# A two-layer hybrid model on one core: the modulation of the second layer beside the grouped attention, and three edits in the scan, its seam and the merge's gates

## What is computed

```python
def adaln(cond, ada_w, ada_b):
    m = jax.nn.silu(cond) @ ada_w + ada_b
    return jnp.split(m, 3, axis=-1)

def modulate(x, gain, shift, scale):
    return rms_norm(x, gain) * (1 + scale) + shift
```

## Time and profile before

| | us |
|---|---|
| median of three runs | 3320.42 |
| lowest, highest | 3320.09, 3335.84 |
| the profiled execution's own time | 3320.01 |
| its span | 3318.2 |
| TensorE busy | 2961.3 (89%) |
| VectorE busy | 1521.4 (46%) |
| ScalarE busy | 1090.3 (33%) |

### The profile page before, as it was taken

How to read it: one execution, slowest core, us unless ns; L and a number is a source line. 1 busy time by engine, 2 the same in 40 slices (tenths; PEclk the granted TensorE clock), 3 DMA queues, 4 the chain that set the end, 5 groups by cost and what they waited for, 6 DMA issues and landing times. The chain is left out here.

```text
span 3318.2 us, 55284 instructions
## 1 busy us (share of the span) xinstructions
PE 2961.3 (89%) x24050; PEld 2254.6 (68%) x24050; DVE 1521.4 (46%) x2488; ACT 1090.3 (33%) x1929; POOL 30.2 (1%) x28
## 2 busy tenths in 40 slices
PE   7799989989986898887899999799887988899998
PEld 3488766867854777445788787566655866788876
DVE  5623247354545344556454424355446435354522
ACT  5411367232253333212322123355323233332221
POOL 0000000000000010000000000000000000000000
PEclk9899999989968999788999998899888999999998
DMA  7511200123113111111233222421212122222321
GB/s 267 151 58 51 49 1 2 51 76 127 33 74 126 42 42 42 35 64 51 64 95 95 86 88 65 129 67 42 77 51 66 33 77 70 70 77 90 97 86 64
DMA packets 246083, 243.36 MB, mean 73 GB/s; under 512 B 28248, under 2 KB 216152, under 8 KB 245777
## 3 DMA queue, kind: packets, MB, share of 16 engines
q1 hardware_dynamic: 245538, 238.64, 23.1%
q10 hardware_dynamic: 304, 1.18, 0.1%
HBM read 217.03 MB, written 22.24 MB: 72 GB/s over the span
## 5 line engine op out<-in xcount | busy, mean ns | idle before, releaser
L201 DVE TENSOR_TENSOR second_w_low<-second_w_raw,second_w_high 128x1024 fp32r<-128x1024 f32 (+1 forms) x228 | 272.4, 1197 | 483.0 <-ACT second_w_high L197 482.4
L197 ACT CAST second_w_high<-second_w_raw 128x1024 fp32r<-128x1024 f32 (+1 forms) x228 | 233.0, 1024 | 689.5 <-PE ffn_in_acc L222 250.9
L220 PE MATMUL ffn_in_acc<-ffn_h_high,second_w_high 128*128 128x512 f32 x704 | 281.1, 399 | 13.9 <-DVE ffn_h_low L578 13.9
L222 PE MATMUL ffn_in_acc<-ffn_h_high,second_w_low 128*128 128x512 f32 x704 | 283.0, 402 | 0.0
L221 PE MATMUL ffn_in_acc<-ffn_h_low,second_w_high 128*128 128x512 f32 x704 | 279.7, 397 | 0.0
L201 DVE TENSOR_TENSOR first_w_low<-first_w_raw,first_w_high 128x1024 fp32r<-128x1024 f32 x115 | 140.1, 1222 | 266.4 <-ACT first_w_high L197 265.7
L197 ACT CAST first_w_high<-first_w_raw 128x1024 fp32r<-128x1024 f32 x115 | 120.2, 1047 | 233.2 <-PE attn_in_acc L222 80.9
L220 PEld LDWEIGHTS ffn_in_acc<-ffn_h_high,second_w_high 128*128 128x128 f32 x704 | 133.5, 190 | 47.8 <-issue 17.1
L220 PE MATMUL attn_in_acc<-attn_h_high,first_w_high 128*128 128x256 f32 (+1 forms) x416 | 144.3, 347 | 14.4 <-DVE attn_h_low L323 14.4
L221 PEld LDWEIGHTS ffn_in_acc<-ffn_h_low,second_w_high 128*128 128x128 f32 x704 | 133.7, 190 | 34.2 <-issue 0.5
L222 PEld LDWEIGHTS ffn_in_acc<-ffn_h_high,second_w_low 128*128 128x128 f32 x704 | 133.6, 190 | 31.1
(11 more groups left out here) (801 smaller groups left out, 6378.3 us busy)
## 6 DMA issues: line engine op xcount, KB each, us to landing
second_w_raw<-in_ffn_w_gate SPq DMA_DIRECT2D x44, 512.0 KB, 3.6
second_w_raw<-in_ffn_w_up SPq DMA_DIRECT2D x44, 512.0 KB, 3.6
second_w_raw<-in_ffn_w_down SPq DMA_DIRECT2D x40, 512.0 KB, 3.4
first_w_raw<-in_rec_w_in SPq DMA_DIRECT2D x33, 512.0 KB, 3.8
first_w_raw<-in_attn_ada_w SPq DMA_DIRECT2D x24, 512.0 KB, 4.7
first_w_raw<-in_rec_ada_w SPq DMA_DIRECT2D x24, 512.0 KB, 5.1
second_w_raw<-in_w_in SPq DMA_DIRECT2D x24, 512.0 KB, 3.7
second_w_raw<-in_w_branch_gate SPq DMA_DIRECT2D x24, 512.0 KB, 3.9
```

What stands on the lines that cost most here:

```text
L197: act.copy(self.view(self.high[b % self.splits], b), self.view(self.raw[b % self.bufs], b)).then_inc(self.high_done, 1)
L201: dve.tensor_tensor(self.view(self.low[b % self.splits], b), self.view(self.raw[b % self.bufs], b), self.view(self.high[b % self.splits], ...
L220: pe.matmul(out, sh, mh, start=(first and j == 0), stop=False)
L222: ins = pe.matmul(out, sl, mh, start=False, stop=(last and j == len(parts) - 1))
```

## The change

Four parts.

1. Only the first layer's adaLN stays in front, in one stage. Its 24 blocks are multiplied in plain f32, unsplit: the weights, 128 x 128, are stationary and silu(cond), two columns, moves; the result lies in PSUM as the modulation needs it. The second layer's 24 blocks ("rec_ada" in the stream, between the attention's input and output weights) are multiplied in the same way beside the grouped attention, one block in each of iterations 0 to 23; iteration 24 makes the first two splits of the output weights, and the modulation.
2. In the scan the square's products come out crossed (the two heads' halves swapped between partitions), so that the units are added by VectorE and not by TensorE; VectorE masks a crossed copy of the diagonal for GpSimd's first inverse, which is made in two halves; units of the later step ("ux") are added by VectorE; y is cleared by GpSimd.
3. At the seam before the scan, two of a unit's four saves are issued earlier, and the last unit's two later saves are waited for only ahead of the scan's second group.
4. The gates are kept in tanh form (g = tanh(a/2), the factor (g + 1) / 2). The eight `gates_first` are opened beside the delta scan, the four last tiles are made beside memory attention, the stage `merge_gates` is gone, and the delta branch's norm runs in `merge0`.

```diff
+def whole_product(pe, w, name, b, ps, silu):
+    b0, view = w.ranges[name][0], w.view(w.raw[b % w.bufs], b)
+    group = 4 * ((b - b0) // 4)
+    pe.wait_ge(w.landed[b % w.bufs], w.landings[b])
+    for j, k in enumerate(w.blocks[b][2]):
+        for i in range(4):
+            ins = pe.matmul(ps[:, group + i, :], view[:, j, i * P:(i + 1) * P], silu[:, k, :],
+                            start=(b == b0 and j == 0 and i == 0), stop=(k == KD - 1), skip_group_check=True)
+    ins.then_inc(w.used_whole, 1)
...
+def adaln(nc, w, cond, silu, layer, gains, aside):
...
+            for b in range(b0, b1):
+                whole_product(pe, w, "adaln", b, ps, silu)
+                aside.pe(pe, b - b0)
...
+            for b in first_splits(w, "attn_in"):
+                w.make_low(dve, b)
+            dve.wait_ge(w.used_whole, w.whole_upto[b1 - 1])
+            modulation(dve, chain, ps, *layer)
...
+class AdaLN:
...
+    def pe(self, pe, i):
+        if self.first + i < self.end:
+            whole_product(pe, self.w, "rec_ada", self.first + i, self.ps, self.silu)
...
+    def dve_last(self, dve, i):
+        if self.first + i == self.end:
+            for b in first_splits(self.w, "attn_out"):
+                self.w.make_low(dve, b)
+            dve.wait_ge(self.w.used_whole, self.w.whole_upto[self.end - 1])
+            modulation(dve, Chain(dve, self.own), self.ps, *self.layer)
...
-            attention(nc, "attn_grouped", pairs, gated(gb, qb), c["ident"])
+            attention(nc, "attn_grouped", pairs, gated(gb, qb), c["ident"], beside=beside)
...
             for n in range(n_units):
                 at = slice((n % 4) * P, (n % 4) * P + P)
+                sp.wait_ge(outs, n + 1)
+                for j in range(2):
+                    sp.dma_start(d["s_feat"][n // 4, j, at, :], out[n % 2][j]).then_inc(saved_out[n % 2], 16)
                 sp.wait_ge(features, n + 1)
...
             for i in range(3):
-                sp.wait_ge(saved_keys[i], 32 * len(range(i, n_units, 3)))
+                sp.wait_ge(saved_keys[i], 32 * len(range(i, n_units - 1, 3)))
...
             def square(n):
                 if n:
-                    pe.wait_ge(act_done, RWKV_ACT(n - 1, "way"))
-                constant(late, 0, all_of(units), 0)
...
+                    pe.wait_ge(act_done, RWKV_ACT(n - 1, "solved"))
+                pe.wait_ge(dve_done, RWKV_DVE(n, "diag"))
+                tiles(late, 0, dt, dn, 0, 1)
+                tiles(late, 256, dn, dt, 0, 1).then_inc(pe_done, 1)
...
             def sixteen(n):
                 pe.wait_ge(dve_done, RWKV_DVE(n, "eight"))
-                constant(early, 0, all_of(units))
                 pe.wait_ge(act_done, RWKV_ACT(n, "m2"))
-                tiles(late, 0, a8, m, 0, 0).then_inc(pe_done, 1)
+                tiles(late, 0, a8, m, 1, 0).then_inc(pe_done, 1)
...
+            def with_units(n, name, to, ps):
+                dve.wait_ge(pe_done, RWKV_PE(n, name))
+                for h in range(2):
+                    dve.tensor_tensor(to[:, :, h].rearrange("p a i t -> p a (i t)"),
+                                      bank(ps, h).rearrange("p (a t) -> p a t", a=2),
+                                      units.rearrange("p a i t -> p a (i t)"), ALU.add).then_inc(dve_done, 1)
...
                     masked(n, gb, "gram_b")
+                    with_units(n, "square", a2, late)
...
-                    odd_half(n, "ux", ux, early)
+                    with_units(n, "ux", ux, early)
...
-            attention(nc, "mem", pairs, [dict(out=branch[2][:, :, t * P:(t + 1) * P]) for t in range(4)], c["ident"], dims=P)
...
+                      beside=InPairs(Beside(w, "gates_last", *u, lambda e, n, ps: rooted(e, last_tile(n), ps, 0.5), 1, last_tile), 2))
...
-            linear(nc, "merge_gates", w, *u, S, lambda e, n, ps: rooted(e, gate(done + n), ps), engines="v",
...
-                ins = dve.tensor_tensor(g, g, ps[:, 0:S], ALU.mult)
+                ins = dve.scalar_tensor_tensor(out=g, in0=g, scalar=1.0, in1=ps[:, 0:S], op0=ALU.add, op1=ALU.mult)
```

More of the change, by code:

```diff
@@ L792, in act @@
             self.product.high(act, i // self.per)
+        if i % self.per == 0 and 1 <= i // self.per <= self.product.tiles and self.product.opened is not None:
+            self.product.treat(act, i // self.per - 1)
     def dve_first(self, dve, i):
@@ new lines, in modulation, with first_splits, _ @@
+def modulation(dve, chain, ps, bias, gain, mod, gs):
+    for j in range(2):
+        chain.link(dve.tensor_tensor(mod[:, :, j], ps[:, :, j], bias, ALU.add))
+        chain.link(dve.tensor_scalar(gs[:, :, j], mod[:, KD:2 * KD, j], 1.0, None, ALU.add))
+        chain.link(dve.tensor_tensor(gs[:, :, j], gs[:, :, j], gain, ALU.mult))
+def first_splits(w, name):
+    first = w.ranges[name][0]
+    return range(first, first + w.split_before(name))
+def adaln(nc, w, cond, silu, layer, gains, aside):
+    b0, b1 = w.ranges["adaln"]
+    with Stage(nc, "adaln") as st:
+        ps = st.ps("acc", [P, 24, 2])
+        silu_done, own = st.sem("silu_done"), st.sem("own")
+        aside.begin(st)
+        block = st.block()
+        @block.sync
+        def _(sp):
+            w.load_stage(sp, "adaln")
+        @block.tensor
+        def _(pe):
+            pe.wait_ge(silu_done, 1)
+            for b in range(b0, b1):
+                whole_product(pe, w, "adaln", b, ps, silu)
+                aside.pe(pe, b - b0)
+        @block.scalar
+        def _(act):
+            act.activation(silu, cond, ACT.Silu).then_inc(silu_done, 1)
+            for b in range(b0, b1):
+                aside.act(act, b - b0)
+            for b in first_splits(w, "attn_in"):
+                w.make_high(act, b, b, None, None)
+        @block.vector
+        def _(dve):
+            chain = Chain(dve, own)
+            dve.tensor_scalar(gains[0], gains[1], 0.125, None, ALU.mult)
+            for b in range(b0, b1):
+                aside.dve(dve, b - b0)
+            for b in first_splits(w, "attn_in"):
+                w.make_low(dve, b)
+            dve.wait_ge(w.used_whole, w.whole_upto[b1 - 1])
+            modulation(dve, chain, ps, *layer)
@@ L2512, in _ @@
             each = eye.rearrange("p (a t) -> p a t", a=1).broadcast_to([P, PAIRS, CH])
-            dve.memset(state[:], 0.0).then_inc(cleared, 1)
-            dve.memset(y[:], 0.0).then_inc(cleared, 1)
+            for dr in range(2):
+                dve.tensor_tensor(near[:, dr, :], chunk[:, 2 * dr, :], same, ALU.mult)
             dve.tensor_scalar(units[:, 0], each, -1.0, None, ALU.mult)
@@ L2518, in _ @@
                 dve.tensor_scalar(twice[:, h], each, 2.0, None, ALU.mult)
-            for dr in range(2):
-                ins = dve.tensor_tensor(near[:, dr, :], chunk[:, 2 * dr, :], same, ALU.mult)
-            ins.then_inc(cleared, 1)
-            dve.wait_ge(cleared, 3)
+            dve.memset(state[:], 0.0).then_inc(cleared, 1)
+            dve.wait_ge(cleared, 1)
             def near_diagonal(n):
@@ L2622, in _ @@
                 dr = groups[n][0]
-                for h in range(2):
-                    act.wait_ge(pe_done, RWKV_PE(n, f"square{h}"))
-                    half(n, "square", a2, late, h)
                 act.wait_ge(pe_done, RWKV_PE(n, "four"))
@@ L3932, in mixer @@
             kept = Ahead(nc, keep, "gates_kept")
-            kept.start(rest[:, 0:GATES_KEPT, :], d["s_gate"].rearrange("(i p) t -> p i t", p=P))
-            done = GATES_FIRST + GATES_KEPT
-            linear(nc, "merge_gates", w, *u, S, lambda e, n, ps: rooted(e, gate(done + n), ps), engines="v",
-                   then=lambda n: lambda act: act.activation(gate(done + n), gate(done + n), ACT.Sigmoid),
-                   aside=Asides(Opened([gate(i) for i in range(GATES_FIRST)], 2), NormAside(c, "dn_out", [branch[1][:, i, :] for i in range(4)], [v("dn_out_norm")] * 4,
-                                          c["pick_mean128"], spread[0:4, :], rs[0:4, :], [out[:, 5, :], out[:, 6, :]], normed,
-                                          dict(square=lambda i: i // 2, sum=lambda i: i // 2, root=1, inverse=1, apply=lambda i: 2 + i // 2),
-                                          finish=lambda dve, i: dve.tensor_tensor(branch[1][:, i, :], branch[1][:, i, :],
-                                                                                  zg[:, i, :], ALU.mult))))
+            kept.start(rest[:], d["s_gate"].rearrange("(i p) t -> p i t", p=P))
@@ new lines, in mixer @@
+            norm_out = NormAside(c, "dn_out", [branch[1][:, i, :] for i in range(4)], [v("dn_out_norm")] * 4,
+                                 c["pick_mean128"], spread[0:4, :], rs[0:4, :], [out[:, 5, :], out[:, 6, :]], normed,
+                                 dict(square=lambda i: i // 2, sum=lambda i: 1 + i // 2, root=3, inverse=3, apply=lambda i: 5 + i // 2),
+                                 finish=lambda dve, i: dve.tensor_tensor(branch[1][:, i, :], branch[1][:, i, :],
```

(3 more changed lines are left out.)

249 lines of the change are left out of this document (126 added, 123 removed).

## The result

The changed kernel takes 3369.14 us (median of four runs, 3358.14 to 3373.21) where the kernel before takes 3325.57 in the runs beside it: ratio 1.0126, interval 1.0104 to 1.0148. It is slower by 1.3%; forecast was no change (3324). The profiled execution took 3370.61 us. The two profiled executions lie 50.6 us apart and the medians 43.6; what follows adds up to the former.

What follows compares the result with a forecast made beforehand. TensorE, busy 89% of the span, was taken as the bound. The terms -7 + 44 - 12 - 7.7 - 13 = +4.3 on a profiled 3320.01 us gave 3324, no change; range 3287 to 3352.

Steps and rivals of the forecast that it cites:

- the narrow pairs: Grouped attention, iterations 16 to 23: each block costs its full 1.98 us at full clock, 15.9 us together.
- Front, -7: Front adaLN: plain f32 products at 1.2 GHz, next stage's first operation at 118.8 instead of 125.55; bounds -42 to -2.
- rival A: Front: the clock rises to full, the part is -42, the sum -31, total 3289; chance 0.12.
- Second layer, +44: Grouped attention: 24 blocks beside it add 40.6 us, the tail in iteration 24 adds 3.4; bounds +25 to +49.
- rival B: Grouped attention: blocks make the clock fall beside iterations 16 to 23, +33, total 3357; chance 0.12 (0.03 for all 24).
- A clock of 0.5 in the grouped attention: Grouped attention: clock forecast at 1.00; a reading of 0.5 was named as showing the prediction wrong.
- the waits on the weights' DMA: Grouped attention: such waits were named as showing the prediction wrong; loads behind bias transfers were forecast to cost 0 to 5.
- rival D: Grouped attention and scan: fifth block queues behind bias transfers (+5), scan gains only 3; sum +18, total 3339; chance 0.12.
- Scan, -12: Scan: removed constants and crossing save 2.2 us in the first group, 0.9 in each other; bounds -30 to -3.
- Seam, -7.7: Between features and scan: block begins some 4 us earlier, first products no longer wait for VectorE's memset and constants.
- my own lower bound: Seam: only -3 if the drain of saves itself sets the loads of chunk and group 0.
- Gates, -13: Mixer: 20.8 beside memory attention, 7.5 norm, 2 waits, 1.8 merge start, against 45 removed; bounds -18 to -6.

Runs made afterwards that it cites:

- ballast: The changed kernel with both runs of eight constant products put back per scan group, overwritten by the real ones; 3364.67 us.
- gates_back: The changed kernel with the mixer's gates as before (sigmoid, the stage of four tiles, nothing beside memory attention); 3366.58 us.
- front_ballast: The changed kernel with one more dense plain f32 matmul of 512 columns in each of the front's 24 blocks, its result unread; 3397.16 us.
- front_rows: The changed kernel with the first layer's adaLN in row form as before, the second layer still beside the grouped attention; 3324.48 us, ratio 0.9997.
- paired: The changed kernel with two second-layer blocks per iteration in iterations 4 to 15, none beside the narrow pairs; 3369.16 us.
- adaln_back: The changed kernel with both layers' adaLN in front as before and nothing beside the grouped attention; 3315.77 us, ratio 0.9971.
- seam_alone: The kernel before with only the seam's earlier saves and later waits, TensorE's wait for y's memset kept; 3320.15 us, ratio 0.9988.
- the other three: The three other kernels with the seam changed and the scan as before; 24.9 to 25.4 us from the features' last matmul to the first gram.
- both_ballast: The changed kernel with adaLN as before and both runs of eight constant products put back in the scan; 3314.31 us.

## Why the prediction was wrong

Three terms failed: the narrow pairs of the grouped attention were sized too small, the scan's gain left out what TensorE pays for its instructions, and the gates' gain was sized too large. The other two came out.

**Front, -7: right, by its mechanism.** -6.1 measured. Plain f32 products in a row stayed at 1.2 GHz for 105 us, as rows 8 and 9 had said, and rival A fell (a rise of some 3 us in ballast and gates_back is all that came of it). The Trainium skill (TensorE: Matmul & The Clock Gate, Part 1: The HAM clock gate) says that "activity releases the throttle"; here TensorE was busy 105.26 of 108 us and loads stayed at 333 ns, so the measurement decides against the plain reading for these products, and front_ballast extends that to one dense f32 matmul per block. What this form costs at this level front_rows tells: in row form the attention's input starts 42 us earlier. Rival A's price was off by its own terms: 48 + 12 and the spread's 3, from 10.3, with the same 2.2 behind, end at 75.5 and not near 83, so it was -50 and not -42.

**Second layer, +44: the term that failed is the narrow pairs.** I had 8 x 1.98 + 3.4 there. The wide part came out cheaper than forecast: iterations 3 to 15 cost 1.32 us each (17.2 for 13, forecast 21.7), as the blocks fill waits for the exponentials; the start cost 4.4 instead of 3. From iteration 16 to the next attention it was 63.8 us against 28.5, +35.3, where the forecast had 19.3. The sixteen microseconds are the clock, which is at 0.50 from 502 on; rival B named this place, though at twice the price (its +33 came on top of the 19.3), and I gave it 0.12 because one stretch of the front, with as many such records among dense ones, was at 1.00. One stretch was too little to set a chance by. paired shows that the blocks do it (take them away and the pairs are back at 2.1 us), and that the wide pairs pay when they get two. A clock of 0.5 in the grouped attention was the prediction's own sign of being wrong; the waits on the weights' DMA, its other one and rival D's, did not come. What decides whether the clock falls isn't settled.

**Scan, -12: the chain gained 9, the instruction supply took 12.** These are means over the traces, so the scan became some 4 us longer; the +10.2 of the table is one pair of executions, and the same crossed scan has stops of 31.8 to 44.9 us from kernel to kernel. Without stops the scan is 8.7 us shorter, three quarters of the forecast. I priced the removed constants as TensorE time and saw no use in them. They were matmuls of 0.24 us where the 64 x 64 ones start 0.02 apart, and while they ran the next packets of instructions came in. Without them TensorE uses up a packet's 127 matmuls sooner and stands until the next is there. The stops of before were in view, "issue" waits of a microsecond or two in each group, and the prediction doesn't speak of them. No view names the packets as the releaser; that the stops wait for them is shown by when they end (451 of 460, above). That slow matmuls relieve them rests on two traces with both kinds put back, 24.5 and 29.9 us, against 31.8 to 44.9.

**Seam, -7.7: right in size, wrong in its larger half.** 28.1 became 20.5. But I gave some 4 of it to SP's earlier start, and seam_alone gained 0.8 there; the saves drain at the same pace whenever they are issued, my own lower bound's reason. What came with the scan's part, the lifted wait on VectorE, gave some 4.5 (25.1 became 20.7, in means of three and of eleven traces). The 2 us between seam_alone and the other three have no reason that the runs show.

**Gates, -13: two terms mis-sized, one missing.** From the memory attention to the end the traces give -15.1 + 16.7 - 5.7 = -4.1, and the times nothing. In memory attention the 96 products took 28 us and not 20.8 (53.4 to the first merge product, less 24 for the attention and 1.8 for the merge's start): two waits of 2 us for the copy of the one bank, a stretch at 1.2 GHz (0.97 in the window), and idle time that they did not fill. Then the merges: +16.7 instead of +9.5. The first merge's products take 35.8 us from first start to last instead of 24.6, with the norm's sums and spreads among them. The norm's last application comes behind the last product, so that the second merge's splits begin late; its wait is 5.3 us of the 11.8, where none was over 3.3 before. And 23.1 us of the merges are at 1.2 GHz where 8.9 were. I had put the norm in merge0 at its TensorE time plus 2 us, and did not follow its chain to the stage's end. This reading is from the trace of the changed kernel; no run took the norm or the bank alone. The missing term is the last stages' -5.7, which hung on nothing that I had looked at.

**The sum.** -7 + 44 - 12 - 7.7 - 13 was +4; in the traces it became -9.5 + 56.8 + 10.2 - 9.4 - 4.1 = +44, and +6.6 stand in stretches that no part touches (+1.4, +5.2). Of the 46 us between, 13 are the grouped attention, 22 the scan, 9 the gates, 7 those stretches, less 4 that front and seam gave more. Part of this is chance: of the scan's 22 a mean pair of traces would have 16. adaln_back's 53 us show that adaLN alone is more than the whole loss. The range ended at 3352, short of B's 3357.

## What to carry to other kernels

Work that moves from a stage limited by its loads to one where TensorE is busy 92% costs most of its TensorE time: here 1.3 us of a block's 2.0 beside the wide pairs. The clock is a price of its own. Here it fell beside iterations of 2.1 us with one block and beside those of 5.0 us with two, so a forecast for such a place needs 1.2 GHz as a case with a real chance. Before slow matmuls are taken out of a long run of very short ones, look for stops on "issue" inside runs of like matmuls, and hold their ends against the packets of the instructions' queue: the slow ones may be giving the instruction supply its time. A norm moved behind a product costs more than its engine time; part of the price stands at the stage's end, where the last application holds up what comes next.

## What the runs showed that I had not expected

- Added work made a stage shorter once: 22 us more of TensorE time in the scan, 8.8 us less length (ballast). In both_ballast the same work made it 6.3 longer.
- TensorE's stops inside runs of like matmuls end 1.15 to 1.7 us after a packet on the instructions' queue has landed, in 451 of 460; a packet serves 127 or 128 matmuls.
- 24 dense f32 matmuls of 512 columns among plain f32 ones left the clock at 1.2 GHz for 146 us (loads of 333 ns); in two kernels with the front unaltered it rose once, for some 3 us, behind the spread's dense matmuls.
- The clock fell beside the narrow pairs with the row form as well (0.72 over 62 us), so the plain f32 form isn't needed for it.
- The windows' granted clock reads 1.00 where the trace has no reading; the length of a weight load, 333 or 192 ns, tells the level.
